# The decay of the state-space scan: from a masked matmul on TensorE to repeated rows, Relu and Exp on ScalarE

## The reference

```python
a_cum = jnp.cumsum(dtc * a.reshape(g, r), axis=2)          # over the 128 tokens of a chunk
seg = a_cum[:, :, :, None] - a_cum[:, :, None, :]
decay = jnp.exp(jnp.where(causal[:, :, None, None], seg, -jnp.inf))
cb = jnp.einsum('bclgn,bcsgn->bclsg', cc, bc)
wts = cb[..., None] * decay * dtc[:, :, None]
y_diag = jnp.einsum('bclsgr,bcsgrp->bclgrp', wts, x)
```

## Time and profile before

| what | value |
|---|---|
| three executions | 5720.52, 5722.25, 5725.28 us |
| the profiled execution, its own time | 5717.07 us |
| its span in the profile | 5715.4 us |
| mean granted TensorE clock | 0.956 of full speed |
| loop of the scan in the trace | about 1344 to 1640 us |
| TensorE, VectorE, ScalarE, GpSimd busy over the whole span | 94%, 51%, 26%, 6% |

### The profile page before, as it was taken

The page is one execution under the profiler, slowest core; times in us unless marked ns, Lnnn a source line. Parts: engine busy times, 40 slices in busy tenths (PEclk is TensorE's granted clock), DMA queues, the critical chain, the costliest instruction groups (busy, mean ns, idle before and its releaser), DMA issues. The chain is left out here.

```text
span 5715.4 us, 70339 instructions
## 1 busy us (share of the span) xinstructions
PE 5380.4 (94%) x25182; PEld 4385.6 (77%) x25182; DVE 2892.6 (51%) x6221; ACT 1459.3 (26%) x2065; POOL 357.0 (6%) x452
## 2 busy tenths in 40 slices
PE   9799999997879879999999999999978999999998
PEld 5578888786755547778888888888867888888887
DVE  5411255104766644345666645555545555555556
ACT  1212233113434432222222222222221111111111
POOL 0100000004730001000000000000000000000000
PEclk9899999899977779999999999999989999999999
DMA  5422233213322245322222224333345555555554
GB/s 200 158 85 96 86 101 115 83 62 110 108 77 93 94 145 166 94 88 93 84 87 92 97 107 159 132 154 139 143 160 149 143 143 143 145 146 145 147 144 132
DMA packets 444041, 692.33 MB, mean 121 GB/s; under 512 B 284657, under 2 KB 300321, under 8 KB 441713
## 3 DMA queue, kind: packets, MB, share of 16 engines
q1 hardware_dynamic: 408002, 556.87, 29.9%
q0 software_dynamic: 32560, 121.00, 6.6%
q10 hardware_dynamic: 3328, 12.58, 0.5%
HBM read 470.02 MB, written 220.36 MB: 121 GB/s over the span
## 5 line engine op out<-in xcount | busy, mean ns | idle before, releaser
L1858 PE MATMUL ph_hid_ps<-ph_n_hi,ph_u_hi 128*128 128x512 f32 x2176 | 855.2, 393 | 8.1 <-DVE ph_u_lo L1991 7.7
L1858 PE MATMUL ph_hid_ps<-ph_n_lo,ph_u_hi 128*128 128x512 f32 x2176 | 847.8, 390 | 0.0
L1858 PE MATMUL ph_hid_ps<-ph_n_hi,ph_u_lo 128*128 128x512 f32 x2176 | 847.7, 390 | 0.0
L2243 PE MATMUL px_out_ps<-px_v_hi,px_weight_hi 128*128 128x512 f32 x2048 | 797.9, 390 | 49.4 <-DVEq L2294 49.4
L2243 PE MATMUL px_out_ps<-px_v_lo,px_weight_hi 128*128 128x512 f32 x2048 | 797.8, 390 | 0.0
L2243 PE MATMUL px_out_ps<-px_v_hi,px_weight_lo 128*128 128x512 f32 x2048 | 797.8, 390 | 0.0
L2322 DVE TENSOR_TENSOR held_tiles<-held_tiles,px_out_ps 128x512 f32<-128x512 f32 x512 | 350.6, 686 | 593.2 <-PE px_out_ps L2243 593.2
L1991 DVE TENSOR_TENSOR ph_u_lo<-ph_u_raw,ph_u_hi 128x1024 fp32r<-128x1024 f32 x136 | 166.7, 1225 | 707.1 <-ACT ph_u_hi L1912 706.8
L2243 PEld LDWEIGHTS px_out_ps<-px_v_hi,px_weight_hi 128*128 128x128 f32 x2048 | 384.9, 188 | 129.6 <-DVEq L2294 49.6
L1858 PEld LDWEIGHTS ph_hid_ps<-ph_n_hi,ph_u_hi 128*128 128x128 f32 x2176 | 409.2, 188 | 92.4 <-DVE ph_u_lo L1991 8.1
L1858 PEld LDWEIGHTS ph_hid_ps<-ph_n_hi,ph_u_lo 128*128 128x128 f32 x2176 | 408.8, 188 | 85.4
(11 more groups left out here) (301 smaller groups left out, 8242.3 us busy)
## 6 DMA issues: line engine op xcount, KB each, us to landing
ph_u_raw<-in_tiles SPq DMA_DIRECT2D x136, 512.0 KB, 3.5
scratch_hidden<-ph_hidden SPq DMA_DIRECT2D x128, 512.0 KB, 2.6
scratch_gate_tiles<-ph_gates SPq DMA_DIRECT2D x16, 4096.0 KB, 12.7
px_v_raw<-in_v_experts SPq DMA_DIRECT2D x128, 512.0 KB, 3.6
px_raw<-scratch_hidden SPq DMA_DIRECT2D x128, 512.0 KB, 5.3
px_gate<-scratch_gate_tiles SPq DMA_DIRECT2D x128, 512.0 KB, 6.5
proj_w_ch<-in_w_ch POOLq DMA_DIRECT2D x62, 512.0 KB, 3.9
mr_w<-in_ada_w POOLq DMA_DIRECT2D x12, 2048.0 KB, 8.8
```

The source lines that it names most:

```text
L1858: mm = pe.matmul(hid_ps[r][:, c * HALF:(c + 1) * HALF], u[r][a][:, k, :], n2[b][:, k, c * HALF:(c + 1) * HALF], start=(k == 0 and a + b == ...
L2243: mm = pe.matmul(out_ps[b][:], weight[q][j][wp][:, t * P:(t + 1) * P], v[q][j][vp][:, c * HALF:(c + 1) * HALF], start=(j == 0 and wp + vp ...
```

## The change

The exponent of the decay no longer comes from a matmul over the masked `da`. The cumulative sums themselves are kept in two forms: `cum`, tokens on the partitions (a copy of the PSUM tile of the first of the three sums, before its Exp), and `cumT`, heads on the partitions, from 8 additional matmuls. `cumT` is stored to HBM. From there SyncE loads, for each group, its 4 rows of 1024 sums into every one of the 128 partitions (`crow`, 2 MB a group). A partition is a token s, a column a token l. ScalarE computes Relu(cum[s] - crow[l]) with the row as input, scale -1 and `cum` as the bias of each partition, one instruction for each of the 4 heads (128 x 128 each), and then, after a wait for these four, Exp(-x) of all four in place. Above the diagonal, where the difference has the other sign, Relu gives 0 and Exp gives 1; the mask in `cb` zeroes that part as before. `spread`, `seg_ps`, the 4 segment matmuls and GpSimd's `spread_da` go. The core of the diff:

```diff
@@ SyncE
+                def load_rows(g, s):
+                    sync.dma_start(crow[s][:], d["cumT"][bass.ds(g * HPG, HPG)].partition_broadcast(P)).then_inc(crow_in[s], 16)
                 for s in range(2):
                     load_group(s, s)
+                sync.wait_ge(cumT_ready, 1)
+                sync.dma_start(d["cumT"], cumT[:]).then_inc(cumT_stored, 16)
+                sync.wait_ge(cumT_stored, 16)
+                for s in range(2):
+                    load_rows(s, s)
                 with sync.Fori(0, TURNS - 1) as i:
                     for s in range(2):
                         sync.wait_ge(y_taken, (2 * i + s) * TT + TT + 2)
                         load_group(2 * i + s + 2, s)
+                        load_rows(2 * i + s + 2, s)
@@ GpSimd
-                def spread_da(g, s, c):
-                    u = g * TT + c
-                    pool.wait_ge(seg_mm, u + 1)
-                    pool.tensor_tensor(spread[c % 2][:], after[:].unsqueeze(1).to_broadcast([P, HPG, P]),
-                                       heads(da, c, g).unsqueeze(2).to_broadcast([P, HPG, P]), ALU.mult).then_inc(spread_ready, 1)
-                    behind(g, s, n, 0, begun, spread_da)
@@ TensorE, ahead of the loop, then in it
-                pe.sem_inc(seg_mm, 2)
+                    if n == 0:
+                        for c in range(TT):
+                            mm = pe.matmul(cumT_ps[:, c * P:(c + 1) * P], da[:, c, :], upto[:], start=True, stop=True)
+                        mm.then_inc(cumT_mm, 1)
-                    pe.wait_ge(spread_ready, u + 1)
-                    pe.wait_ge(decay_ready, u + 1)
-                    for r in range(HPG):
-                        mm = pe.matmul(seg_ps[b][:, r, :], spread[b][:, r, :], upto[:], start=True, stop=True)
-                    mm.then_inc(seg_mm, 1)
@@ ScalarE, ahead of the loop, then in it
+                    if n == 0:
+                        act.activation(cum[:], sums_ps[:], ACT.Copy).then_inc(cum_ready, 1)
+                        act.wait_ge(cumT_mm, 1)
+                        act.activation(cumT[:], cumT_ps[:], ACT.Copy).then_inc(cumT_ready, 1)
                     act.activation(out[:], sums_ps[:], ACT.Exp).then_inc(sums_exp, 1)
+                act.wait_ge(cum_ready, 1)
-                    act.wait_ge(seg_mm, u + 3)
+                    if c == 0:
+                        act.wait_ge(crow_in[s], (g - s) * 8 + 16)
                     act.wait_ge(weights_ready, u + 1)
-                    act.activation(decay[b][:], seg_ps[b][:], ACT.Exp).then_inc(decay_ready, 1)
+                    for r in range(HPG):
+                        fall = act.activation(decay[b][:, r, :], crow[s][:, r, c * P:(c + 1) * P], ACT.Relu, scale=-1.0,
+                                              bias=cum[:, c, bass.ds(g * HPG + r, 1)])
+                    fall.then_inc(fall_ready, 1)
+                    act.wait_ge(fall_ready, u + 1)
+                    act.activation(decay[b][:], decay[b][:], ACT.Exp, scale=-1.0).then_inc(decay_ready, 1)
```

More of the change, by code:

```diff
@@ L1012, in stage_ssd @@
     OUTS = 4
+    d["cumT"] = nc.dram_tensor("scratch_cumT", (SH, S), F32, kind="Internal").ap()
     ROOT, NORM, OUT = 1, 2, 3
@@ L1018, in stage_ssd @@
         after = sp.sb("after", [P, P])
+        cum = sp.sb("cum", [P, TT, SH])
+        cumT = sp.sb("cumT", [SH, S])
+        crow = [sp.sb(f"crow{s}", [P, HPG, S]) for s in range(2)]
         ones = sp.sb("ones", [P, P])
@@ L1033, in stage_ssd @@
         rows = [sp.sb(f"rows{b}", [P, HALF]) for b in range(2)]
-        spread = [sp.sb(f"spread{b}", [P, HPG, P]) for b in range(2)]
         x_dt = [sp.sb(f"x_dt{b}", [P, HPG, HD]) for b in range(2)]
@@ L1049, in stage_ssd @@
         turn_ps = [sp.ps(f"turn_ps{b}", [P, HALF]) for b in range(2)]
-        seg_ps = [sp.ps(f"seg_ps{b}", [P, HPG, P]) for b in range(2)]
+        cumT_ps = sp.ps("cumT_ps", [SH, S])
         y_ps = [sp.ps(f"y_ps{b}", [P, 2, HPG, HD]) for b in range(2)]
@@ L1062, in stage_ssd @@
         turn_taken = sp.sem("turn_taken")
-        spread_ready = sp.sem("spread_ready")
-        seg_mm = sp.sem("seg_mm")
+        cum_ready = sp.sem("cum_ready")
+        cumT_mm = sp.sem("cumT_mm")
+        cumT_ready = sp.sem("cumT_ready")
+        cumT_stored = sp.sem("cumT_stored")
+        crow_in = [sp.sem(f"crow_in{s}") for s in range(2)]
+        fall_ready = sp.sem("fall_ready")
         decay_ready = sp.sem("decay_ready")
```

## The result

The changed kernel takes 5755.82 us (median of 5 runs, 5749.91 to 5763.06), the kernel before 5723.53 us (5 runs, 5720.52 to 5726.89). The ratio is 1.0057 (1.0042 to 1.0072): slower, by 32.3 us between the medians, and by more than the 0.2% that counts as no change. The forecast was 5750 us. The profiled execution of after has a span of 5753.9 us at clock 0.948, that of before 5715.4 us at 0.956.

A forecast was written before the change was run, and what follows sets the result against it. It took the scan step to be bound by a TensorE-VectorE loop of 4.56 us. Start +17.5, seven groups +11.2 and group 0 -0.3 gave +28.4 on 5717.07 us, 5745.5; with medians 5.2 higher, 5750 us, range 5732 to 5795.

The forecast's parts named there:

- The sum: Scan stage: 17.5 us at its start, 11.2 in seven groups, less 0.3 in group 0, together +28.4 us.
- Table and Relus: ScalarE's added work a step: four Relus 1.28 us, Exp 0.63 us, no added table load.
- Inside a group: Scan steps after a group's first ones: period 4.5 us (4.4 to 4.8), 0.05 less than before.
- B: Scan step's closing loop, TensorE's outputs, then VectorE's state, scaled, weights: 4.56 us before, 4.48 forecast.
- D: Scan step's loop through ScalarE, yz to rows to decay to weights: 1.4 us slack before, 4.48 us forecast.
- Steps 0 to 2: First three steps of groups 1 to 7, decay having less slack: +1.1, +0.55 and +0.25 us.
- Step 3: Step of groups 1 to 7 holding VectorE's normalisation of the group before: 0 to -0.3 us, taken as -0.1.
- The groups: Groups 1 to 7 of the scan: +1.6 us each, +11.2 us for seven.
- rival 1: TensorE's clock falls in the scan's gaps: 58 us more if half the units run cold, 5808 us; chance 0.16.
- The start: Head of the scan, waiting for the cumT store and first crow rows: +17.5 us, bounds +8 and +21.
- small start: At the scan's start the store overtakes the loads, +8 us, groups at lower bound, +1: 5731 us; chance 0.07.
- rival 3: Relief wins in the scan: decay found ready, GpSimd no longer slowing VectorE, steps 4.2 us, total 5709; chance 0.06.

The follow-up runs named there:

- one_relu: Changed kernel with one 128x512 Relu a chunk instead of four 128x128, one head's bias serving all four: 5746.42 us, ratio 1.0042.
- kept_matmuls: Changed kernel with 4 matmuls a unit put back where the segment sums were, result unused: 5753.92 us, ratio 1.0050.
- store_other_queue: Changed kernel with the small cumT store issued from ScalarE's queue, row loads staying in SyncE's: 5754.63 us, ratio 1.0061.
- start_order: Changed kernel with SyncE loading group 0, storing cumT and loading group 0's rows before group 1's loads: 5749.44 us, ratio 1.0042.
- removal_only: Kernel before with spread and segment matmuls done once ahead of the loop, nothing added, most decays wrong: 5725.59 us, ratio 1.0012.
- early_rows: Changed kernel with copy rows waiting for y_mm instead of y_taken, and GpSimd's y_taken wait gone: 5726.33 us, ratio 1.0009.

## Why the prediction was right

It was right in sign and near in size. The step, the groups and the start came out by the terms given; two reasons under them did not hold, and they are named.

- *The sum.* Forecast +28.4 us in the stage, measured +30.4: 16.1 at the start, 13.9 in groups 1 to 7, 0.4 in the rest.
- *Table and Relus.* 1.28 for four, measured 1.26 to 1.28; Exp 0.63, measured 0.63; no table load.
- *Inside a group.* Forecast 4.48 by two loops of equal length, measured 4.48. That B holds it alone is shown by `one_relu`; that D was as long, only by the trace of after. I gave `weights` 0.68 and `state` no gain; they are 0.74 and 0.65 (0.72 in the earlier trace rows), and that the errors cancel is luck.
- *Steps 0 to 2.* Forecast 4.13, 4.5 and 5.76, measured 4.10, 4.34 (4.6 where TensorE was cold) and 5.70.
- *Step 3.* Forecast -0.1. Measured 5.95 warm, unchanged to within 0.1, and 6.44 cold.
- *The groups.* +1.6 a group forecast; with the clock held (`kept_matmuls`) +1.55 measured. In after it is 2.0. The rest is rival 1, at 3.1 us and not its 58: the clock falls for single steps between the long waits of steps 0 to 2, where the forecast looked only inside a group. Of the signs, the granted clock of 1.00 failed: it is 0.90 from 1365 to 1630 and 0.89 from 1360 to 1664, just at the 0.9 below which I called myself wrong. ScalarE's wait for `yz` is 1.0 us a unit shorter and not 1.3.
- *The start.* Forecast +17.5, measured +16.1. The rows land at 1362.08, on the scale of before 1360.55 (forecast 1361.9), and from there to the third `rows` it is 8.07 us (forecast 8.2). Two errors lie inside this: the store was through 0.7 us later than forecast, and the rows took 7.1 us and not 8.8. One reason under this term was wrong. I held the store's place behind 6 MB to be what decides, and put the lower bound at +8 if it did not wait. The store did wait, 11.5 us. The Trainium skill, "DMA: Bandwidth & Descriptors", section "Queues, rings and completion order", says that descriptors are consumed in ring order on each DMA engine, and the trace agrees. But `store_other_queue` shows that 1.7 us hang on the store's place. The case "small start" was not to be had in that way; only fewer bytes ahead of the rows bring it (`start_order`, -7.9).
- *Relief of VectorE* (rival 3). In the warm group of `removal_only` steps 0 to 3 gain 0.7 us, where the rival had 1.3, and steps 4 to 7 together 0.3, where it had 0.36 each: `state` stayed at 0.65 without `spread`. The clock took back what there was.

Open: each trace is of one execution. Which steps are cold differs from group to group in it; whether also from execution to execution, and so what the clock costs in the median, wasn't measured.

## What to carry to other kernels

Before work is moved from one engine to another, find which wait closes the step: here the work removed from TensorE and GpSimd was on no loop, while that added to ScalarE used up 1.3 of the 1.4 us of slack inside a group and set steps 0 to 2, where there was less. Ask of each wait in that loop whether it guards what it must; `rows` waited for `yz` where the end of TensorE's reading was enough. With GpSimd's wait of the same kind this was worth 27 us, most of what the whole change had cost. And a transfer that the first step needs goes ahead of the prefetch of the next group: here its time was that of the bytes in front of it.

## What the runs showed of the hardware

- VectorE's `state` (two inputs, 128 x 256) takes 0.42 us alone and 0.65 to 0.73 beside GpSimd's products of the same size. Which instructions meet is set by waits elsewhere, so moving one wait on ScalarE and one on GpSimd (`early_rows`) made VectorE faster.
- An activation of 128 x 128 with a bias for each partition costs 390 ns, one of 128 x 512 costs 710 ns: four of the first in a row are 1.27 us (`after`, `one_relu`), so 0.56 us is the price of four instructions in place of one.
- TensorE at 194 us of 265 busy, with waits of 1.6 to 2.6 us in three steps running (`after`), was granted 0.90 of its clock; at 226 of 265 (`kept_matmuls`) it was 0.97. A cold step 3 is 0.5 us longer in `after` (6.44 instead of 5.95) and 1.4 in `early_rows` (7.02 instead of 5.66), where the next step gives 0.7 back (3.49 instead of 4.21); one cold step in `removal_only` 1.9 us (6.35 instead of 4.48).
